# Six of the eight block products of each MLP as seven half-width products of a Strassen scheme

## The chip, the cores and the metric

The kernel runs on one core of a Trainium2 chip. The metric is the device time of one execution in microseconds. Five engines work side by side and meet only at semaphores: TensorE (PE, with its weight loads listed as PEld), VectorE (DVE), ScalarE (ACT), GpSimd (POOL), and SyncE (SP), which issues the weight transfers.

## The reference

A stack of transformer layers over 512 tokens of width 1024: two mixers of a first block, then a second block of two layers, each with a mixer and an MLP, and a last norm. All of it is fp32. The change touches only the two MLPs of the second block:

```
def sq_relu_mlp(h, w_up, w_down):            # w_up 1024 x 4096, w_down 4096 x 1024
    u = jnp.einsum('btd,df->btf', h, w_up)
    return jnp.einsum('btf,fd->btd', jnp.square(jax.nn.relu(u)), w_down)

h = h + sq_relu_mlp(rms_norm_2(h, mlp_norm_g[layer]), mlp_w_up[layer], mlp_w_down[layer])
```

## The kernel before

The activations lie in SBUF transposed: X holds the residual as 8 tiles of 128 features by 512 tokens. A matrix product in nearly full fp32 precision is made of three fp32r matmuls: each operand is split into a high part (rounded to fp32r) and a low part (the rest), and `three` issues high·high, low·high and high·low (L288, L289, L290) into one PSUM bank.

An MLP is cut into four chunks of 1024 hidden features. A chunk is one "up" product (1024 x 1024 weights on HH and HL, the normed input) and one "down" product (1024 x 1024 weights on the hidden tiles). So one MLP is eight block products, in the order up 0, up 1, down 0, up 2, down 1, up 3, down 2, down 3. Each product is 8 output tiles (`tile_t`), each tile 8 tiles of the contraction times 3 matmuls: 24 matmuls of 128x128 weights by 512 columns. L is the layer, c the chunk, m the tile.

Each output tile needs one block of weights of 128 x 1024 values (512 KB). SP loads it into one of two buffers WRAW (`load`); ACT rounds it to WH (`split_high`, L256); DVE subtracts to WL (`split_low`, L265). Both wait until TensorE has used the block three before, so a block is made ready within the time of the tiles ahead of it.

For an up tile DVE evicts relu(bank)·RS to TMP (L2293), ACT squares it and rounds it to a high part (L2316, L2320), and POOL subtracts to get the low part (L2339). For a down tile DVE adds the bank to X (`add_x`, L482). Eight PSUM banks are taken in turn. The up product of the next chunk stands between an up product and the down product that reads its hidden tiles.

Each engine runs its instructions strictly in the order in which its function (`mlp_tensor`, `mlp_vector`, `mlp_scalar`, `mlp_gpsimd`) issues them. SP takes the blocks in the order of a list, `plan`.

Of the kernel before, what the change touches and what calls it, by code (L numbers as in the profile page):

```python
# [8 lines left out]
F32 = mybir.dt.float32  # L9
# [6 lines left out]
T = 512  # L16
# [8 lines left out]
NR, NS = 2, 3  # L25
LAMBDA_INIT = 0.8 - 0.6 * math.exp(-0.3)
# [9 lines left out]
for _n, _w in (("l0", 8), ("l1", 8), ("qa", 2), ("kva", 1), ("qn", 1), ("qr", 1), ("qrs", 1), ("kn", 1), ("kr", 1),  # L36
# [3 lines left out]
    GAIN_W += _w  # L40

# [92 lines left out]
def program(nc, A, out):  # L134
    ctx = ExitStack()
    with ctx:
# [7 lines left out]

        HH = sb("HH", [128, KT, T], FR)
        HL = sb("HL", [128, KT, T], FR)
        WH = [sb(f"WH{i}", [128, BW], FR) for i in range(NS)]
        WL = [sb(f"WL{i}", [128, BW], FR) for i in range(NS)]
# [4 lines left out]
        (yout,) = alias([("yout", [128, KT, T], F32)])  # L153
# [26 lines left out]
        HIDH0, HIDL0, HIDH1, HIDL1 = alias([(f"HID{i}", [128, KT, T], FR) for i in range(4)])  # L180
        HID = [(HIDH0, HIDL0), (HIDH1, HIDL1)]
# [4 lines left out]
        sb("SHARED", [128, 21568])  # L186

        X = sb("X", [128, KT, T])
        WRAW = [sb(f"WRAW{i}", [128, BW]) for i in range(NR)]
        SCR = sb("SCR", [128, 3 * 1280])  # L190
        ST = sb("ST", [128, 512])
# [6 lines left out]
        TMP = sb("TMP", [128, 4, T])  # L198
        EPSC = sb("EPSC", [128, 7])
        ACC = sb("ACC", [128, T])  # L200
        EHH, EHL = sb("EHH", [128, 2, 62], FR), sb("EHL", [128, 2, 62], FR)
# [3 lines left out]
        TRI = sb("TRI", [128, 256], FR)  # L205
# [30 lines left out]
        stream = A["plan"]  # L236
# [4 lines left out]
        on_pool |= {block[("o_v", b), half] for b in range(1, 4) for half in range(2)}  # L241

        def load(e, w, b):
            if b >= NR:
                w.wait_ge(*at("low", b - NR))
            name, i, width, _ = stream[b]
            e.dma_start(WRAW[b % NR][:, 0:width], A[name][i]).then_inc(*dma(f"s_w{b % NR}"))

        def split_high(e, w, b):
# [4 lines left out]
            if b >= NS:  # L254
                w.wait_ge(*at("used", b - NS))
            e.activation(WH[b % NS][:, 0:n], WRAW[b % NR][:, 0:n], ACT.Copy).then_inc(*inc("s_high", ("high", b)))  # L256

# [74 lines left out]
        def h_lo(k):  # L332
# [1932 lines left out]
        def up_tiles(e, w, L, c, g):  # L2265
            for m in range(8):
# [1004 lines left out]
```

## Time and profile before

| | before |
|---|---|
| median of 3 runs | 1849.88 us (1848.64 to 1854.93) |
| the profiled execution | 1848.76 us, its span 1847.0 us |
| PE busy | 1804.7 us, 98% of the span |
| DVE, ACT, POOL busy | 53%, 43%, 26% |
| granted TensorE clock, mean | 0.998 |
| HBM traffic | 77 GB/s over the span |

The span runs from the first to the last instruction; the 1.8 us between it and the execution's time lie around it. Matmuls are pipelined: the duration listed for one is from its start to its modelled end, and matmuls overlap, so their rate is read from the distance between two starts. "Idle before" is the time in which an engine had nothing under way ahead of an instruction, with the instruction that released it.

### The profile page before, as it was taken

The numbers are of one execution on the slowest core, as the hardware profiler recorded it, in microseconds if no ns is written. First come the engines' busy times: TensorE is split into PE (matmuls) and PEld (weight loads), VectorE is DVE, ScalarE is ACT, GpSimd is POOL, SyncE is SP. The second block draws the span as 40 slices with busy tenths as digits, with TensorE's granted clock in tenths as the row PEclk, the third lists the DMA queues.
The fourth block names the chain that finished last, engine by engine and source line by source line (L and its number), as shares of the span: only waits on it lengthen the run. The fifth ranks groups of instructions, "written<-read, shape, count | busy, mean of one in ns | idle before, by whom it ended". The sixth has DMA issues, their size and how long they took to land.

```text
span 1847.0 us, 24633 instructions
## 1 busy us (share of the span) xinstructions
PE 1804.7 (98%) x9664; PEld 1441.0 (78%) x9668; DVE 981.4 (53%) x1581; ACT 797.4 (43%) x1401; POOL 476.5 (26%) x475
## 2 busy tenths in 40 slices
PE   7999999999999999999999999999999999999997
PEld 6987777776678766677888888888888788888886
DVE  5355556575546688854433434365677653333333
ACT  5236665455435365564441423233445543232412
POOL 0035551101312145560120201005677112010200
PEclk9999999999999999999999999999999999999999
DMA  5221111231012311012222222222222122222222
GB/s 182 93 71 54 48 46 60 82 97 48 23 57 96 124 65 34 30 36 70 91 102 103 92 92 102 103 91 81 81 86 75 57 92 100 96 97 97 95 98 79
DMA packets 44514, 149.10 MB, mean 81 GB/s; under 512 B 6000, under 2 KB 6384, under 8 KB 44400
## 3 DMA queue, kind: packets, MB, share of 16 engines
q1 hardware_dynamic: 44400, 147.53, 23.6%
q8 instruction: 78, 1.28, 0.3%
q14 instruction: 36, 0.29, 0.1%
HBM read 139.64 MB, written 2.10 MB: 77 GB/s over the span
## 4 chain that ended last, share of the span: by engine, by line
PE 87%; DVE 5%; POOL 3%; ACT 3%; issue 2%; DMA 1%; POOLq 0%; SPq 0%; DVEq 0%; ACTq 0%
PE BANK L288 23%; PE BANK L290 22%; PE BANK L289 22%; PE BANK L920 3%; PE BANK L654 2%; PE BANK L1704 1%; PE BANK L1685 1%; PE BANK L1661 1%; PE BANK L977 1%; PE BANK L2499 1%; PE BANK L639 1%; PE BANK L2474 1%; DVE LH L763 1%; POOL LH L885 1%; PE BANK L2462 1%
## 5 line engine op out<-in xcount | busy, mean ns | idle before, releaser
L256 ACT ACTIVATE WH<-WRAW 128x1024 fp32r<-128x1024 f32 x262 | 273.3, 1045 | 452.0 <-PE BANK L290 425.6
L265 DVE TENSOR_TENSOR WL<-WRAW,WH 128x1024 fp32r<-128x1024 f32 (+1 forms) x249 | 326.6, 1312 | 253.1 <-ACT WH L256 252.2
L288 PE MATMUL BANK<-HH,WH 128*128 128x512 f32 x1048 | 422.4, 403 | 11.1 <-DVE WL L265 9.6
L290 PE MATMUL BANK<-HL,WH 128*128 128x512 f32 x1048 | 409.4, 391 | 0.0
L289 PE MATMUL BANK<-HH,WL 128*128 128x512 f32 x1048 | 408.9, 390 | 0.0
L288 PEld LDWEIGHTS BANK<-HH,WH 128*128 128x128 f32 x1048 | 197.4, 188 | 60.5 <-issue 20.6
L290 PEld LDWEIGHTS BANK<-HL,WH 128*128 128x128 f32 x1048 | 197.1, 188 | 42.0
L289 PEld LDWEIGHTS BANK<-HH,WL 128*128 128x128 f32 x1048 | 197.6, 189 | 40.4 <-issue 2.9
L2339 POOL TENSOR_TENSOR HID<-TMP,HID 128x512 fp32r<-128x512 f32 x64 | 82.8, 1293 | 527.1 <-ACT HID L2320 527.1
L288 PE MATMUL BANK<-HID,WH 128*128 128x512 f32 (+1 forms) x520 | 200.8, 386 | 0.0
L290 PE MATMUL BANK<-HID,WH 128*128 128x512 f32 (+1 forms) x520 | 200.6, 386 | 0.0
L289 PE MATMUL BANK<-HID,WL 128*128 128x512 f32 (+1 forms) x520 | 200.6, 386 | 0.0
L482 DVE TENSOR_TENSOR X<-X,BANK 128x512 f32<-128x512 f32 x95 | 65.3, 687 | 230.5 <-PE BANK L290 230.5
L2316 ACT ACTIVATE TMP<-TMP 128x512 f32<-128x512 f32 x64 | 40.5, 632 | 202.7 <-DVE TMP L2293 202.7
L288 PEld LDWEIGHTS BANK<-HID,WH 128*128 128x128 f32 x520 | 97.7, 188 | 19.7
L290 PEld LDWEIGHTS BANK<-HID,WH 128*128 128x128 f32 x520 | 97.7, 188 | 19.7
L289 PEld LDWEIGHTS BANK<-HID,WL 128*128 128x128 f32 x520 | 97.7, 188 | 19.6
L2293 DVE SCALAR_TENSOR_TENSOR TMP<-BANK,RS 128x512 f32<-128x512 f32 x64 | 44.2, 690 | 59.4 <-PE BANK L290 59.3
L875 POOL TENSOR_TENSOR L0P<-TMP,L0P 128x512 fp32r<-128x512 f32 x16 | 35.3, 2205 | 146.0 <-DVE L0P L750 146.0
L885 POOL TENSOR_TENSOR LH<-SCR,LH 128x512 fp32r<-128x512 f32 (+1 forms) x48 | 54.0, 1124 | 41.7 <-DVE LH L763 41.7
L2104 ACT ACTIVATE SCR<-BANK,ST 128x512 f32<-128x512 f32 (+3 forms) x96 | 49.6, 525 | 20.1 <-DVE ST L1885 19.9
L2774 ACT ACTIVATE SCR<-BANK,ST 128x128 f32<-128x128 f32 (+3 forms) x64 | 33.1, 522 | 56.8 <-DVE ST L2639 56.8
(413 smaller groups left out, 3113.6 us busy)
## 6 DMA issues: line engine op xcount, KB each, us to landing
WRAW<-in_w SPq DMA_DIRECT2D x77, 512.0 KB, 3.4
WRAW<-in_wu SPq DMA_DIRECT2D x64, 512.0 KB, 3.2
WRAW<-in_wd SPq DMA_DIRECT2D x64, 512.0 KB, 3.2
WRAW<-in_w0o SPq DMA_DIRECT2D x8, 512.0 KB, 3.5
WRAW<-in_w1o SPq DMA_DIRECT2D x8, 512.0 KB, 3.4
WRAW<-in_wc SPq DMA_DIRECT2D x8, 512.0 KB, 3.2
WRAW<-in_w2o SPq DMA_DIRECT2D x8, 512.0 KB, 3.2
WRAW<-in_w3o SPq DMA_DIRECT2D x8, 512.0 KB, 3.2
```

The costliest lines, as they stand in the source:

```text
L256: e.activation(WH[b % NS][:, 0:n], WRAW[b % NR][:, 0:n], ACT.Copy).then_inc(*inc("s_high", ("high", b)))
L265: e.tensor_tensor(WL[b % NS][:, 0:n], WRAW[b % NR][:, 0:n], WH[b % NS][:, 0:n].bitcast(F32), ALU.subtract).then_inc(*inc("s_low_pool" if p ...
L288: e.matmul(dst, ah, bh, start=first and i == 0, stop=False)
L289: e.matmul(dst, al, bh, start=False, stop=False)
L290: made = e.matmul(dst, ah, bl, start=False, stop=last and i == len(sets) - 1)
L482: e.tensor_tensor(X[:, m, :], X[:, m, :], banks[name, m], ALU.add).then_inc(*inc("s_evac", ("evac", name, m)))
L885: e.tensor_tensor(LH1[:, h % 2, c], l0_buf[h % 3][:, c], LH0[:, h % 2, c].bitcast(F32), ALU.subtract).then_inc(*inc("s_fail_lo", ("fail lo ...
L920: made = e.matmul(bank[:, c], a, b, start=(i == 0), stop=(i == len(sets) - 1), skip_group_check=True)
L2104: e.activation(e_exp(u)[:, b, 0:n], BANK[2 * (u % 2) + b][:, 0:n], ACT.Exp, bias=e_stat(u, b), accum_out=e_stat(u, 2 + b)).then_inc(*inc(" ...
L2293: e.scalar_tensor_tensor(out=TMP[:, t % 4, :], in0=banks[("up", L, c), m], scalar=0.0, in1=RS[:, :], op0=ALU.max, op1=ALU.mult).then_inc(* ...
L2316: e.activation(t, t, ACT.Square).then_inc(*inc("s_hid", ("hid square", L, c, m)))
L2339: e.tensor_tensor(lo[:, m, :], TMP[:, (8 * c + m) % 4, :], hi[:, m, :].bitcast(F32), ALU.subtract).then_inc(*inc("s_hid_lo", ("hid lo", L, ...
```

## The change

In each MLP the products up 0 and down 3 stay as they are; the six between them run in the order down 0, up 1, down 1, up 2, down 2, up 3 and by another scheme. Such a product takes its weights, its input and its output as 2x2 blocks (feature tiles k and k+4, output tiles m and m+4, token halves of 256) and computes the 2x2 block product with seven block products in place of eight (a Strassen scheme in Winograd's form).

A step (`FAST`, 48 per MLP) is one pair of output tiles (m, m+4) and one half of the contraction. Per step:

- SP loads the four weight quarters of 128 x 256 (512 KB in all) into one of three buffers RAW (`fast_load`).
- POOL makes four sums of 256 columns from them (`fast_sums`). The second waits for the first, the fourth for the second.
- ACT rounds seven operands of 256 columns in one instruction of 1792 columns (`fast_high`); DVE subtracts in one of 1792 (`fast_low`). RAW and the split operands G have three buffers each.
- TensorE runs 7 products times 2 tiles times 3 matmuls of 256 columns (`fast_pe`), 42 in all, into four banks of a pair; two pairs share the eight banks in turn.

After both steps of a pair, ACT copies one product out of PSUM (256 columns, `first_act`) and DVE joins the seven products in four instructions (512, 512, 256 and 512 columns, `join_vec`) in the one buffer Q. For a down pair POOL adds two tiles of 512 to X (`add_pool`). For an up pair DVE makes relu and square in one pass of 1024 columns (`relu_vec`); the input sums of the next down product come from POOL in three instructions of 512, 256 and 256 (`hid_mix`), then ACT rounds 1792 columns and DVE subtracts 1792 (`hid_high`, `hid_low`). Hidden planes of chunk 3 need no sums and are 1024 wide. The input of the up products, X·gain·RS, is staged and summed once per MLP in four planes (`stage_vec`, two DVE instructions of 512; `plane_mix` like `hid_mix`; `plane_high`, `plane_low`, 1792 columns each): two planes during up 0, two during down 0.

The up 0 tiles run in the order 0, 4, 1, 5, 2, 6, 3, 7, and the product after them is down 0, where before it was up 1. The square of up 0 stays on ACT.

```
+        def fast_sums(e, w, L, s):
...
+            w.wait_ge(*dma(f"s_raw{s % 3}", L * NF // 3 + s // 3 + 1))
+            a21, a11, a12, a22, s1, s3, s2, s4 = (raw_part(s, i) for i in range(8))
+            e.tensor_tensor(s1, a21, a22, ALU.add).then_inc(*inc("s_fast_sum", ("first sum", L, s)))
+            e.tensor_tensor(s3, a21, a11, ALU.subtract).then_inc(*inc("s_fast_sum", ("third sum", L, s)))
+            w.wait_ge(*at("first sum", L, s))
+            e.tensor_tensor(s2, s1, a11, ALU.subtract).then_inc(*inc("s_fast_sum", ("second sum", L, s)))
+            w.wait_ge(*at("second sum", L, s))
+            e.tensor_tensor(s4, a12, s2, ALU.subtract).then_inc(*inc("s_fast_sum", ("sums", L, s)))
...
+        def fast_low(e, w, L, s):
...
+            w.wait_ge(*at("fast high", L, s))
+            e.tensor_tensor(flat(fast_w(s)[:, 7:14, :]), raw_part(s, 1, 7), flat(fast_w(s)[:, 0:7, :]).bitcast(F32),
+                            ALU.subtract).then_inc(*inc("s_fast_low", ("fast low", L, s)))
+        def turn_pool(e, w, S, *key):
+            e.tensor_tensor(S[:, 0:2, :], S[:, 7:8, :].broadcast_to([128, 2, 256]), S[:, 5:7, :], ALU.subtract).then_inc(
+                *inc("s_mixed", ("first mix", *key)))
...
+            e.tensor_tensor(S[:, 2, :], S[:, 5, :], S[:, 1, :], ALU.subtract).then_inc(
+                *inc("s_mixed", ("second mix", *key)))
...
+            e.tensor_tensor(S[:, 3, :], S[:, 4, :], S[:, 2, :], ALU.subtract).then_inc(
+                *inc("s_mixed", ("mixed", *key)))
...
+        def fast_pe(e, w, L, s):
...
+            w.wait_ge(*at("fast low", L, s))
+            wh, wl = fast_w(s)[:, 0:7, :], fast_w(s)[:, 7:14, :]
+            started = set()
+            for name in LATE if kind == "dn" and pair < 2 and half else FIRST:
+                a, b, j, side = PRODUCTS[name]
+                for i in range(2):
...
+                    e.matmul(dst, wh[:, a, cols], hi, start=half == 0 and j not in started, stop=False, skip_group_check=True)
+                    started.add(j)
+                    e.matmul(dst, wl[:, a, cols], hi, start=False, stop=False, skip_group_check=True)
+                    made = e.matmul(dst, wh[:, a, cols], lo, start=False, stop=half == 1 and i == 1, skip_group_check=True)
...
+        def relu_vec(e, w, L, c, p):
...
+            q = flat(Q[:, 0:4, :])
+            e.scalar_tensor_tensor(out=flat(D[:, 4:8, :]), in0=q, scalar=0.0, in1=q, op0=ALU.max, op1=ALU.mult).then_inc(
+                *inc("s_hid_square", ("hid square", L, c, p)))
+
+        def add_pool(e, w, L, c, p):
...
+            e.tensor_tensor(X[:, p + 4, :], X[:, p + 4, :], flat(Q[:, 0:2, :]), ALU.add).then_inc(*inc("s_x_added"))
+            e.tensor_tensor(X[:, p, :], X[:, p, :], flat(Q[:, 2:4, :]), ALU.add).then_inc(
+                *inc("s_x_added", ("x added", L, c, p)))
```

The loop over the steps s on DVE and POOL, in the order of issue ("now", "last", "before" and "third" are the pairs that ended at step s, s-1, s-2 and s-3):

```
+            for s in range(NF + 1):
+                now, last, before, third = (ended.get(s - i, ("", 0, 0)) for i in range(4))
+                if last[0]:
+                    join_vec(e, w, L, *last, 3)
+                if third[0] == "up" and third[1] < 3 and third[2] < 3:
+                    hid_low(e, w, L, *third[1:])
+                if last[0] == "up":
+                    relu_vec(e, w, L, *last[1:])
...
+                fast_low(e, w, L, s + 2)
...
+                if now[0]:
+                    for i in (1, 2, 4):
+                        join_vec(e, w, L, *now, i)
...
+            for s in range(NF + 1):
+                last = ended.get(s - 1, ("", 0, 0))
+                fast_sums(e, w, L, s + 3)
+                if s == 0:
+                    hid_mix(e, w, L, 0, 3)
+                if last[0] == "up" and last[1] < 3:
+                    hid_mix(e, w, L, *last[1:])
+                if last[0] == "dn":
+                    add_pool(e, w, L, *last[1:])
+                if s in (2, 4):
+                    plane_mix(e, w, L, s // 2 + 1, D)
```

## Rows read from the trace of the kernel before

**Rows 1.** The page: busy time by engine, and the granted clock in 40 slices.

```profile
PE 1804.7 (98%) x9664; PEld 1441.0 (78%) x9668; DVE 981.4 (53%) x1581; ACT 797.4 (43%) x1401; POOL 476.5 (26%) x475
PEclk9999999999999999999999999999999999999999
```

**Rows 2.** The page: the chain that ended last, shares by engine.

```profile
PE 87%; DVE 5%; POOL 3%; ACT 3%; issue 2%; DMA 1%; POOLq 0%; SPq 0%; DVEq 0%; ACTq 0%
```

**Rows 3.** Windows over the first MLP: busy PE, PEld, DVE, ACT, POOL, clock, DMA.

```profile
879.20:966.20 87.00, 87.00 (x384) 71.63 (x383) 39.05 (x41) 36.76 (x50) 19.42 (x15) 1.00 0.26 91
966.20:1009.70 43.50, 43.50 (x194) 36.02 (x193) 15.55 (x16) 9.64 (x10) 1.29 (x1) 1.00 0.31 109
...
1140.20:1183.70 43.50, 43.50 (x193) 36.02 (x192) 15.55 (x16) 9.64 (x10) 1.29 (x1) 1.00 0.31 109
```

**Rows 4.** Timeline of TensorE, end of the second MLP: 512 columns, then 256.

```profile
1821.88 0.39 PE L290 MATMUL BANK<-HID,WH 128*128 128x512 f32 x1
...
1829.36 0.39 PE L290 MATMUL BANK<-HID,WH 128*128 128x512 f32 x1
1829.59 0.28 PE L288 MATMUL BANK<-HID,WH 128*128 128x256 f32 x1
...
1833.78 0.28 PE L290 MATMUL BANK<-HID,WH 128*128 128x256 f32 x1
```

**Rows 5.** Timelines of TensorE and DVE: start of up 0, first eviction.

```profile
878.39 0.39 PE L288 MATMUL BANK<-HH,WH 128*128 128x512 f32 x1
...
889.76 0.69 DVE L2293 SCALAR_TENSOR_TENSOR TMP<-BANK,RS 128x512 f32<-128x512 f32 x1
```

**Rows 6.** Instructions of single lines: duration in ns, least, median, most.

```profile
L265 DVE TENSOR_TENSOR WL<-WRAW,WH x249: 407/1226/2353, 8.3 to 1820.1; 128x1024 fp32r<-128x1024 f32 x121, 128x704 fp32r<-128x704 f32 x4
L482 DVE TENSOR_TENSOR X<-X,BANK x95: 680/687/690, 299.4 to 1829.8; 128x512 f32<-128x512 f32 x95
L2339 POOL TENSOR_TENSOR HID<-TMP,HID x64: 1290/1290/1307, 891.9 to 1750.3; 128x512 fp32r<-128x512 f32 x64
L2320 ACT ACTIVATE HID<-TMP x64: 631/632/633, 891.1 to 1749.6; 128x512 fp32r<-128x512 f32 x64
```

**Rows 7.** Groups by line and shape, with mean ns of one.

```profile
L256 ACT ACTIVATE WH<-WRAW 128x1024 fp32r<-128x1024 f32 x65 | 68.4, 1053 | 127.0 <-PE BANK L290 127.0
L455 DVE TENSOR_TENSOR RS<-RS,TMP 128x512 f32<-128x512 f32 x1 | 0.7, 692 | 0.0
```

**Rows 8.** Timeline, DVE and POOL: a DVE instruction with one SBUF input beside POOL.

```profile
1836.39 2.10 POOL L2993 TENSOR_TENSOR yout<-yout,RS 128x256 f32<-128x256 f32 x3 [84.80 <-ACT RS L2967]
1836.74 2.04 DVE L2983 SCALAR_TENSOR_TENSOR yout<-X,GC,BANK 128x256 f32<-128x256 f32 x5
```

**Rows 9.** Timeline, DVE and POOL: DVE instructions with two SBUF inputs beside POOL.

```profile
133.62 1.21 DVE L265 TENSOR_TENSOR WL<-WRAW,WH 128x1024 fp32r<-128x1024 f32 x1
133.77 1.65 POOL L885 TENSOR_TENSOR LH<-SCR,LH 128x256 fp32r<-128x256 f32 x1 [0.23 <-DVE LH L763]
...
187.21 1.23 DVE L265 TENSOR_TENSOR WL<-WRAW,WH 128x1024 fp32r<-128x1024 f32 x1
187.29 2.28 POOL L875 TENSOR_TENSOR L0P<-TMP,L0P 128x512 fp32r<-128x512 f32 x1 [4.21 <-DVE L0P L750]
...
1350.24 1.28 POOL L2855 TENSOR_TENSOR TMP<-TMP,ROPE 128x512 f32<-128x512 f32 x1
1350.42 2.18 DVE L265 TENSOR_TENSOR WL<-WRAW,WH 128x1024 fp32r<-128x1024 f32 x1
1351.47 2.28 POOL L2881 TENSOR_TENSOR OG3L<-OX,OG3H 128x512 fp32r<-128x512 f32 x1
```

**Rows 10.** The page: DMA issues of the MLP weights, us to landing.

```profile
WRAW<-in_wd SPq DMA_DIRECT2D x64, 512.0 KB, 3.2
```

**Rows 11.** Windows where TensorE is partly idle.

```profile
603.00:606.00 3.00, 2.40 (x17) 1.88 (x16) 2.45 (x2) 0.42 (x1) 2.87 (x3) 1.00 0.51 175
1836.00:1840.00 4.00, 1.50 (x8) 0.69 (x6) 3.39 (x9) 2.01 (x5) 2.62 (x4) 1.00 0.00 0
```

More of the change, by code:

```diff
@@ new lines, in mlp_tensor, with part @@
+            for s in range(NF):
+                fast_pe(e, w, L, s)
+            def part(m, ks):
+                b = block[("dn", L, 3), m]
+                wh, wl = (x[b % NS][:, 0:BW].rearrange("p (k n) -> p k n", k=KT) for x in (WH, WL))
+                w.wait_ge(*at("high", b))
+                w.wait_ge(*at("low", b))
+                if ks[0] == 0:
+                    _, was = banks.take((("dn", L, 3), m), ("evac", ("dn", L, 3), m))
+                    for key in was:
+                        w.wait_ge(*at(*key))
+                made = three(e, w, banks[("dn", L, 3), m],
+                             [(wh[:, k, :], wl[:, k, :], dn_plane(k, 0), dn_plane(k, 1), [("hid lo", L, 3, k % 4)]) for k in ks],
+                             ks[0] == 0, ks[-1] == 7)
+                if ks[-1] == 7:
+                    made.then_inc(*inc("s_tile", ("tile", ("dn", L, 3), m), ("used", b)))
@@ L2304, in mlp_vector @@
+            hid_low(e, w, L, 3, 3)
+            split_low(e, w, block[("dn", L, 3), 2], False)
             if L == 0:
@@ new lines, in mlp_scalar @@
+            for s in range(NF + 1):
+                now, last, before = (ended.get(s - i, ("", 0, 0)) for i in range(3))
+                if s == 1 or before[0] == "up" and before[1] < 3 and before[2] == 3:
+                    hid_high(e, w, L, before[1], 3, 1)
+                fast_high(e, w, L, s + 2)
+                if s >= NF - 1:
+                    split_high(e, w, block[("dn", L, 3), s - NF + 1])
+                if s == 0 or last[0] == "up" and last[1:] != (3, 3) and last[2] == 3:
+                    hid_high(e, w, L, last[1], 3, 0)
+                if before[0] == "up" and (before[2] < 3 or before[1] == 3):
+                    hid_high(e, w, L, *before[1:])
+                if s in (3, 5):
+                    plane_high(e, w, L, (s + 1) // 2, D)
+                if now[0]:
+                    first_act(e, w, L, *now)
@@ L3035, in sync @@
             o_swaps = {block[o_slots[s]] + NS + NR: s for s in o_swapped}
-            for b in range(NR, len(stream)):
+            for _, _, _, key in plan[NR:]:
+                if key[0] == "fast":
+                    fast_load(e, w, *key[1:])
+                    continue
+                b = block[key]
                 for pair in m_swaps.get(b, ()):
```

391 lines of the change are left out of this document (306 added, 85 removed).

## The prediction

> **What bounds the kernel now.** I read the page's busy times first: PE is busy 98% of the span and nothing else over 53%, at full clock in every slice [rows 1]. The chain that ended last runs through PE for 87% [rows 2]. Windows over the first MLP show PE without a gap: each block product of 8 tiles takes 43.5 us, so a tile takes 5.44 us, while DVE works 15.6 to 17 us and POOL 1.3 to 9 us of such a window [rows 3]. So an MLP costs what its matmuls cost. Their rate is the distance between starts, not the listed duration: 33 matmuls of 512 columns from 1821.88 to 1829.36 are 0.2267 us each; 35 of 256 columns from 1829.59 to 1833.78 are 0.1197 us [rows 4]. Twice the columns cost 1.89 times as much, so halving the width loses a little.
>
> **TensorE after the change.** A step has 42 matmuls of 256 columns: 42 x 0.1197 = 5.03 us, where an old tile is 24 x 0.2267 = 5.44 us. There are 96 steps in the two MLPs, so if TensorE stays the bound the change gives 96 x 0.41 = 39 us and no more. TensorE no longer hides as much, though, so the question is whether the others keep up with 5.03 us a step, 10.06 us a pair.
>
> By the Trainium skill, "TensorE: Matmul & The Clock Gate", section "Back-to-back issue gap", a matmul costs its columns at the full clock plus a small constant, 109 ns for 256 and 216 ns for 512 columns; by that page's figures the step would save 0.59 us, 57 us in all. The rows of this case say less, and they decide.
>
> **What the helpers do in a step.** Durations first. DVE with both inputs in SBUF: 1.226 us for 1024 columns [rows 6], 0.692 for 512 [rows 7], that is 1.043 ns a column; so 1792 columns take 2.03. POOL: 1.29 us for 512 columns [rows 6], three of 256 in 2.10 us, 0.70 each [rows 8]. ACT: 0.632 for 512, 1.053 for 1024 [rows 6, 7], so 1.68 for 1792.
>
> - ACT, per up pair: two weight roundings, one hidden rounding, one copy under 0.63: at most 5.7 of 10.06 us. Hidden.
> - DVE, per up pair: two `fast_low` and a `hid_low` of 2.03, `relu_vec` 1.23, joins of 1792 columns from PSUM in four instructions, 0.69 for each of 512 [rows 6] and some 0.4 for that of 256: 6.09 + 1.23 + 2.5 = 9.8 us. Just under TensorE, if nothing else holds it. A down pair has 6.6.
> - POOL: eight sums of 0.70 = 5.6; plus `hid_mix` 1.29 + 2 x 0.70 = 2.69, or `add_pool` 2 x 1.29 = 2.58: 8.3 us a pair. Also under.
> - DMA: the same 512 KB per step as per tile, 3.2 us to land [rows 10], three buffers. The engines' share was 0.24 to 0.31 [rows 3]. Nothing changes.
>
> Each engine alone would fit. But DVE and POOL do not run side by side here. When a DVE instruction with two SBUF inputs meets a POOL instruction that reads SBUF, the second one stands still until the first is over [rows 9]: DVE from 187.21 to 188.44, and POOL, started at 187.29, ends 2.28 us later where it needs 1.29, that is 1.13 after DVE's end. At 1350.24 POOL, DVE and POOL come in turn: POOL ends 1351.52, DVE 1.08 later (its 1024 columns), the next POOL instruction 1.15 after that. In the whole trace I found over a hundred such meetings, and none in which the two overlapped. DVE instructions with one SBUF input are free of it: five with a PSUM input beside three of POOL, both at their usual pace [rows 8]. Before, the meetings are rare and lie under PE. The change puts almost all of its new work on these two engines: sums, mixes, additions to X on POOL; subtractions and the relu (both inputs Q, in SBUF) on DVE. Only the joins, which read PSUM, go beside POOL.
>
> So the sum that counts is the time in which one of the two excludes the other. Behind a POOL instruction, a DVE one costs 0.15 less than alone: 1.08 for 1024 columns, 1.88 for 1792, 0.54 for 512. A POOL one behind DVE costs 0.14 less (1.15 for 1.29). I take the first for all DVE instructions, and the second once per DVE instruction.
>
> - Down pair: 5.6 + 2 x 1.88 + 2.58 - 2 x 0.14 = 11.7 us.
> - Up pair (up 1, up 2): 5.6 + 3 x 1.88 + 1.08 + 2.69 - 4 x 0.14 = 14.5 us.
> - Before, the two tiles: 10.88 us. TensorE's part now: 10.06 us.
>
> Both kinds of pair are bound by DVE and POOL together.
>
> **The sum for one MLP**, from the first eviction. That comes 11.4 us after up 0 has begun, since it waits for the norm's factor [rows 5]; this part is not changed.
>
> - During up 0: five mixes 13.5; seven subtractions of 1792 (three hidden planes, two input planes, steps 0 and 1) 13.2; staging of two planes 2.2; five `split_low` 5.4; sums of three steps 8.4: 42.7 us.
> - After it: sums of 45 steps 126.0; 46 `fast_low` 86.5; 12 `add_pool` 31.0; eight up pairs' mix, relu, subtraction 5.65 each, 45.2; four pairs of up 3 with 1024 columns twice 8.6; input planes 2 and 3 11.3; the last plane of up 0 4.6: 313.2 us.
> - Less 0.14 for each of 94 DVE instructions: 13.2. Total 342.7 us.
>
> Before, this stretch (first eviction to the start of down 3) is 7 x 43.5 = 304.5 less 11.4: 293.1 us. The difference is 49.6 us. Two terms are not in it. The work is not wholly without idle: at each of the three hand-overs to a down product the last hidden plane goes through a join, the plane before it, relu, mix behind a step's sums, rounding and subtraction, 0.69 + 2.03 + 1.23 + 2.69 + 2.8 + 1.68 + 2.03 = 13.2 us against two steps of cover, 10.1, so some 3.1 us each, 9.4; dependent POOL instructions leave short gaps, 80 of them, no row of before shows this pair of operations, and I take 0.05 each, 4 us. And the last step's matmuls outlast the helpers by about 2. So 49.6 + 9.4 + 4 + 2 = 65 us per MLP, 130 for both: 1848.8 + 130 = **1979 us**, against the profiled execution's 1848.76, which is 1.1 below the median of 1849.88.
>
> The down 3 product should lose nothing: its first block waits for step 46, the second for the last step, rounding 1.05 and subtraction 1.23 behind join and relu come 3.5 us after it, under the first part's 18 matmuls, 4.1 us. The wait of SP for `fast low` 47 in front of these loads holds only blocks that are needed a step later.
>
> **The ends.** Low: every POOL instruction (264 per MLP, not 94) costs 0.14 less and nothing idles: 24 less, so 49.6 - 24 + 2 = 28 per MLP, 1904 us. High: full durations on both sides (94 x 0.29 = 27 more) and twice the idle (27): 49.6 + 27 + 27 + 2 = 106 per MLP, 2060 us. I take the middle values since the two engines will mostly wait in turn, and that is what the row at 1350.24 shows.
>
> By the Trainium skill, "SBUF — State Buffer", section "Who interferes with whom", the pair of ports is held exclusively for the whole of an instruction. Taken literally, whole durations add, which is my high end without the extra idle; the rows agree with the exclusion but show 0.14 to 0.15 us of each instruction outside it, and I go by them.
>
> **Rivals.**
>
> *TensorE stays the bound* (the other side: faster). If a wide subtraction and a short POOL sum could interleave, each engine alone fits: 9.8 and 8.3 us under 10.06. Then 1848.8 - 39 = 1809, plus some 5 us at each down 0, whose hidden planes had a whole up 1 as cover before and have none now: 1819 us. For it: busy shares of 53% and 26%. Against it: rows 9. It decides from the point where the excluded time per MLP, 343 + 15, falls under 293, that is if 65 us of it can overlap. 0.12.
>
> *A draw*: part of it overlaps and ends about where it was, 1850. 0.03.
>
> *The single buffer D*: relu of the next plane waits until this one is mixed, rounded and subtracted. Unhindered the loop is 1.23 + 2.69 + 1.68 + 2.03 = 7.6 us, but `fast_low` (2.03) and a step's sums (2.8) stand in the two queues and DVE and POOL exclude each other inside it, up to some 17 us a pair in place of 14.5: eight pairs x 2.5 x 2 MLPs = 40 us more, 2019. Inside my range. 0.10.
>
> *The clock*: TensorE would idle a fifth of the time in these stretches (5.03 of about 6.3 us a step). At 1.2 GHz 256 columns are 213 ns and a step 9.0 us: 96 x (9.0 - 5.44) = +342, some 2190 us. Against it: at 80% and at 38% busy the granted clock stayed 1.00 [rows 11]. 0.03.
>
> *The forecast*: 0.72.
>
> **Range and chances.** Forecast and D together hold 0.82 between 1904 and 2060; the range is 1900 to 2060. A measurement of this kernel tells 0.3% from no change, 5.5 us. Faster 0.12, same 0.03, slower 0.85.
>
> **What the profile after would show.** PE busy well under 98%, its gaps in front of the first matmul of a step with `fast_low` on DVE as releaser; 42 matmuls 0.12 apart inside a step; up products longer than down products, some 58 against 47 us; `fast_low` at about 2.03 us at best with a mean above 2.4; POOL sums with a mean over 0.8 and some near 2.6, when they stand behind a subtraction; DVE's joins at their usual 0.69. The clock at 1.00. I am wrong if PE runs through the fast products without gaps, if sums and subtractions overlap at their own durations, or if the waits in front of a step name the DMA or ACT.

## The result and the profile after

The changed kernel took 1995.25 us (median of four runs, 1994.8 to 1996.09), the kernel before 1849.41 (median of four): 1.078 times as long, with an interval of 1.0761 to 1.0803, 146 us more. The forecast was 1979 (1900 to 2060), slower with a chance of 0.85.

The page of the changed kernel, busy times, then the granted clock in 40 slices, and the chain that ended last by engine:

```profile
PE 1827.0 (92%) x11392; PEld 1529.3 (77%) x11396; DVE 1263.5 (63%) x1763; ACT 868.2 (44%) x1383; POOL 1037.2 (52%) x939
...
PEclk9999999999999999998988989999999979899999
...
PE 51%; POOL 26%; DVE 13%; ACT 5%; issue 4%; DMA 1%; DVEq 0%; POOLq 0%; SPq 0%; ACTq 0%
```

Beside [rows 1] and [rows 2]: PE fell from 98% to 92% of a longer span, POOL's busy time more than doubled, and POOL and DVE, 8% of the chain before, now make 39% of it. No single helper is full: 63% and 52%. Only their sum is large, and in the MLPs it is above 100% where busy time includes waiting for each other.

Windows of the first MLP, one for each product from up 0 to up 3 (up 2 and down 2, 54.60 and 51.85 us long, repeat up 1 and down 1). Columns: stretch, length, busy time of PE, PEld, DVE, ACT, POOL, granted clock, DMA share, GB/s.

```profile
881.50:945.84 64.34, 47.58 (x196) 37.36 (x194) 39.45 (x35) 24.48 (x25) 36.77 (x31) 0.89 0.21 69
945.84:996.73 50.89, 43.97 (x337) 43.63 (x337) 36.78 (x28) 20.09 (x17) 48.95 (x38) 0.90 0.23 73
996.73:1051.21 54.48, 45.02 (x336) 44.29 (x337) 37.99 (x30) 17.83 (x13) 51.21 (x43) 0.91 0.26 78
1051.21:1103.09 51.88, 45.80 (x337) 45.06 (x338) 35.38 (x28) 16.70 (x15) 49.78 (x43) 0.90 0.25 82
...
1209.54:1257.24 47.70, 42.73 (x339) 42.01 (x337) 35.72 (x32) 16.98 (x16) 32.44 (x28) 0.96 0.27 86
```

Every product took 43.5 us before [rows 3], up 0 some 44.5 with the matmuls for the norm's factor in it. The six products of an MLP that have 42 matmuls a step now take 47.7 to 54.6 us, where 8 x 5.03 = 40.3 would do for TensorE, and POOL is busy for 94 to 96% of the windows from down 0 to down 2. The product ahead of them, up 0, whose matmuls are not changed, takes 64.3.

From the start of up 0 (881.49) to the start of down 3 (1257.24) the first MLP needs 375.8 us, against 305.6 before (878.39 to 1183.98): +70.2. The second needs 374.6, against 305.6: +69.0. Up 0 of the first MLP starts 3.1 us later than before, 2.7 us are lost between the start of the first down 3 and the second up 0, and 1.1 behind the start of the second down 3 (56.5 us to the end, against 55.5). 3.1 + 70.2 + 2.7 + 69.0 + 1.1 = 146.

The costliest groups that bear on it: busy total, mean ns of one, idle before them and its releaser. `fast_low` is L2361, the fourth of `fast_sums` L2344, the first L2339, the first operation of the mixes L2365, the first addition to X L2525, relu L2516, the joins L2491 to L2499.

```profile
L2361 DVE TENSOR_TENSOR G<-RAW,G 128x1792 fp32r<-128x1792 f32 x96 | 229.6, 2406 | 95.8 <-ACT G L2354 95.7
L2354 ACT ACTIVATE G<-RAW 128x1792 fp32r<-128x1792 f32 x96 | 163.2, 1700 | 270.2 <-POOL RAW L2344 254.8 <-PE BANK L2460 15.4
L2344 POOL TENSOR_TENSOR RAW<-RAW 128x256 f32<-128x256 f32 x96 | 144.2, 1502 | 7.5
L2339 POOL TENSOR_TENSOR RAW<-RAW 128x256 f32<-128x256 f32 x96 | 100.4, 1046 | 0.0
L2365 POOL TENSOR_TENSOR TMP<-TMP 128x512 f32<-128x512 f32 x28 | 65.4, 2334 | 144.9 <-ACT TMP L2627 129.8 <-DVE TMP L2516 13.9 <-DVE TMP L2383 1.3
L2525 POOL TENSOR_TENSOR X<-X,Q 128x512 f32<-128x512 f32 x24 | 45.3, 1887 | 0.0
L2516 DVE SCALAR_TENSOR_TENSOR TMP<-Q 128x1024 f32<-128x1024 f32 x24 | 35.0, 1460 | 1.7
L2491 DVE TENSOR_TENSOR Q<-Q,BANK 128x512 f32<-128x512 f32 x48 | 33.0, 688 | 4.2
```

The means tell who meets whom. A POOL sum of 256 columns needs 0.70 us [rows 8] and the fourth one takes 1.50 on average; where it takes 2.4, as at 1137.11 below, a subtraction on DVE runs beside it. POOL's 512 columns need 1.29 [rows 6] and take 2.33 and 1.89. DVE's 1792 columns, 2.03 at best, take 2.41, and the relu 1.46 for 1.23. The joins, one input in PSUM, stay at 0.69. ACT, which rounds what the POOL has summed, waits 254.8 us for that fourth sum.

The timeline of an up pair in up 2, DVE and POOL in order of time:

```profile
1134.90 0.69 DVE L2491 TENSOR_TENSOR Q<-Q,BANK 128x512 f32<-128x512 f32 x1
...
1139.02 1.56 DVE L2516 SCALAR_TENSOR_TENSOR TMP<-Q 128x1024 f32<-128x1024 f32 x1
1140.50 5.03 DVE L2361 TENSOR_TENSOR G<-RAW,G 128x1792 fp32r<-128x1792 f32 x2
...
1134.89 0.74 POOL L2339 TENSOR_TENSOR RAW<-RAW 128x256 f32<-128x256 f32 x1
...
1137.11 2.38 POOL L2344 TENSOR_TENSOR RAW<-RAW 128x256 f32<-128x256 f32 x1
1140.65 2.99 POOL L2365 TENSOR_TENSOR TMP<-TMP 128x512 f32<-128x512 f32 x1 [1.16 <-DVE TMP L2516]
1143.72 2.40 POOL L2368 TENSOR_TENSOR TMP<-TMP 128x256 f32<-128x256 f32 x1
1146.20 0.73 POOL L2371 TENSOR_TENSOR TMP<-TMP 128x256 f32<-128x256 f32 x1
```

This is [rows 9] again, now in a steady rhythm. Two subtractions take 5.03 us together instead of 4.06, and the 256 columns that start at 1143.72 beside the second of them take 2.40, where the next ones, with DVE idle, take 0.73. A join and a POOL sum that start together, at 1134.9, both keep their own durations (0.69 and 0.74). So the sentence at the start of this document, that the engines meet only at semaphores, does not hold for DVE and POOL.

The chain that ended last, over a down pair (from the addition to X of down 1's third pair to that of its fourth, which runs on POOL while TensorE has begun up 2) and an up pair in up 2 (start, us, what):

```profile
1102.82 1.25 POOL X L2525
1104.07 1.26 POOL X L2526
1105.33 2.48 POOL RAW L2339
...
1112.21 2.39 POOL RAW L2344
1114.61 1.26 POOL X L2525
...
1134.11 0.70 DVE Q L2486
...
1136.64 2.28 DVE HID L2424
...
1139.02 1.57 DVE TMP L2516
...
1140.65 3.00 POOL TMP L2365
...
1145.53 3.49 issue
1149.02 0.70 DVE Q L2486
```

A down pair is POOL from end to end, 11.8 us (1102.82 to 1114.61), two of its ten POOL instructions stretched to 2.4 by a subtraction; an up pair is 14.9 us (1134.11 to 1149.02), passed back and forth between the two engines. In the first MLP no piece of the chain belongs to TensorE from 888.13, under up 0, to 1245.61, in the last quarter of up 3.

From the timeline one can also add up the time in which neither a POOL instruction nor a DVE instruction with two SBUF inputs is under way. An instruction that stands still while the other works adds nothing to such a union, so what is left over is what the pair of engines, taken as one, has free:

| stretch | length, us | free for both, us |
|---|---|---|
| up 0 from the first eviction (892.96 to 945.84) | 52.9 | 8.0 |
| down 0, up 1, down 1 | 50.9, 54.5, 51.9 | 0.9, 0.6, 0.4 |
| up 2, down 2 | 54.6, 51.9 | 0.6, 0.4 |
| up 3 | 47.7 | 5.4 |

In the five products in the middle the two engines together are full to 98 or 99%, at 63% and 52% busy each over the span.

### The profile page after: what moved, and what is told of

It is laid out like the page before. It is cut to its first block, busy times and chain, and to the rows that moved or that the text cites. A ratio compares the mean times of both kernels' runs of the same rounds, so it can differ in the third digit from the quotient of the medians.

```text
span 1993.0 us, 28779 instructions
## 1 busy us (share of the span) xinstructions
PE 1827.0 (92%) x11392; PEld 1529.3 (77%) x11396; DVE 1263.5 (63%) x1763; ACT 868.2 (44%) x1383; POOL 1037.2 (52%) x939
## 4 chain that ended last, share of the span: by engine, by line
PE 51%; POOL 26%; DVE 13%; ACT 5%; issue 4%; DMA 1%; DVEq 0%; POOLq 0%; SPq 0%; ACTq 0%
PE BANK L314 11%; PE BANK L316 10%; PE BANK L315 10%; POOL RAW L2344 5%; POOL RAW L2339 4%; POOL RAW L2342 3%; POOL TMP L2365 3%; POOL RAW L2340 2%; PE BANK L948 2%; PE BANK L682 2%; DVE HID L2424 2%; POOL X L2526 2%; POOL X L2525 2%; POOL TMP L2368 2%; PE BANK L1732 1%
## 5 line engine op out<-in xcount | busy, mean ns | idle before, releaser
L314 PE MATMUL BANK<-HH,WH 128*128 128x512 f32 x664 | 278.3, 419 | 18.1 <-DVE WL L291 9.3
L282 ACT ACTIVATE WH<-WRAW 128x1024 fp32r<-128x1024 f32 (+2 forms) x166 | 172.4, 1041 | 270.7 <-PE BANK L316 225.6
L2361 DVE TENSOR_TENSOR G<-RAW,G 128x1792 fp32r<-128x1792 f32 x96 | 229.6, 2406 | 95.8 <-ACT G L2354 95.7
L2354 ACT ACTIVATE G<-RAW 128x1792 fp32r<-128x1792 f32 x96 | 163.2, 1700 | 270.2 <-POOL RAW L2344 254.8
L2457 PE MATMUL BANK<-HID,G 128*128 128x256 f32 x672 | 202.4, 301 | 72.8 <-DVE TMP L2568 25.5
L316 PE MATMUL BANK<-HL,WH 128*128 128x512 f32 x664 | 264.8, 399 | 0.0
L291 DVE TENSOR_TENSOR WL<-WRAW,WH 128x1024 fp32r<-128x1024 f32 (+2 forms) x153 | 192.7, 1260 | 102.4 <-ACT WH L282 101.1
L2457 PE MATMUL BANK<-HP,G 128*128 128x256 f32 x672 | 197.9, 295 | 46.5 <-DVE G L2361 43.5
L2459 PE MATMUL BANK<-HID,G 128*128 128x256 f32 x672 | 199.7, 297 | 0.0
L2460 PE MATMUL BANK<-HID,G 128*128 128x256 f32 x672 | 199.3, 297 | 0.0
L2457 PEld LDWEIGHTS BANK<-HID,G 128*128 128x128 f32 x672 | 139.0, 207 | 77.8 <-issue 32.5
L2459 PE MATMUL BANK<-HP,G 128*128 128x256 f32 x672 | 195.6, 291 | 0.0
L2460 PE MATMUL BANK<-HP,G 128*128 128x256 f32 x672 | 195.0, 290 | 0.0
L314 PEld LDWEIGHTS BANK<-HH,WH 128*128 128x128 f32 x664 | 126.6, 191 | 56.5 <-issue 28.5
L2344 POOL TENSOR_TENSOR RAW<-RAW 128x256 f32<-128x256 f32 x96 | 144.2, 1502 | 7.5
L2365 POOL TENSOR_TENSOR TMP<-TMP 128x512 f32<-128x512 f32 x28 | 65.4, 2334 | 144.9 <-ACT TMP L2627 129.8
L2459 PEld LDWEIGHTS BANK<-HID,G 128*128 128x128 f32 x672 | 139.0, 207 | 0.0
L2460 PEld LDWEIGHTS BANK<-HID,G 128*128 128x128 f32 x672 | 138.9, 207 | 0.0
```

The source lines that it names most:

```text
L291: e.tensor_tensor(WL[b % NS][:, 0:n], WRAW[b % NR][:, 0:n], WH[b % NS][:, 0:n].bitcast(F32), ALU.subtract).then_inc(*inc("s_low_pool" if p ...
L314: e.matmul(dst, ah, bh, start=first and i == 0, stop=False)
L316: made = e.matmul(dst, ah, bl, start=False, stop=last and i == len(sets) - 1)
L2344: e.tensor_tensor(s4, a12, s2, ALU.subtract).then_inc(*inc("s_fast_sum", ("sums", L, s)))
L2354: e.activation(flat(fast_w(s)[:, 0:7, :]), raw_part(s, 1, 7), ACT.Copy).then_inc(*inc("s_fast_high", ("fast high", L, s)))
L2361: e.tensor_tensor(flat(fast_w(s)[:, 7:14, :]), raw_part(s, 1, 7), flat(fast_w(s)[:, 0:7, :]).bitcast(F32), ALU.subtract).then_inc(*inc("s_ ...
```

## The experiments

The kernel before took 1849 to 1850 us beside each. e1 and e2 were timed once; for the others the ratio to the kernel before is given with its interval. The edits are against the changed kernel. Product lengths are of the first MLP. "Free" is the time defined above.

**e1: the same instructions with one input in SBUF.** The first question was whether it is the two SBUF inputs that cost, or the mere number of instructions, waits and hand-overs.

```diff
-            e.tensor_tensor(flat(fast_w(s)[:, 7:14, :]), raw_part(s, 1, 7), flat(fast_w(s)[:, 0:7, :]).bitcast(F32), ALU.subtract)...
+            if s < 3:
+                ...                                   # the subtraction, as it was, and return
+            ...                                       # a wait for the step before
+            e.tensor_reduce(BEHIND[:, 0:7], RAW[s % 3][:, 1:8, :], AX.X, ALU.add)...
...
+            if c in (1, 2):                           # in hid_low
+                e.tensor_reduce(BEHIND[:, 8:8 + n], D[:, cut, :], AX.X, ALU.add)...
```

> The subtraction of the weights' low parts (from step 3 on) and that of the hidden low parts of chunks 1 and 2 are replaced on VectorE by a reduction over the same 1792 columns: the low parts stay what they were, so the output is not the reference's. Length, order and waits on VectorE stay, but the instruction has one SBUF input where it had two. Exclusion theory (an instruction with two SBUF inputs and one of GpSimd stand still for each other): GpSimd's sums fall to 0.73 us each, both kinds of pair become bound by TensorE at 10.1 to 10.5 us where down pairs took 13 and up pairs 13.6, some 65 us less per MLP, about 1865 us in all. Rival, VectorE alone has too much to do or the chain of hand-overs is too long: nothing changes, since every duration stays, about 1995 us. Rival, GpSimd alone is the bound: its idle time stays near zero and the time stays above 1950 us.

Measured: 1865.04 us. The groups of DVE's reduction and of two of the sums, and the windows of up 1 and down 1:

```profile
L2367 DVE TENSOR_REDUCE JUNK<-RAW 128x7 f32<-128x1792 f32 x90 | 181.5, 2017 | 52.9 <-ACT G L2355 51.4
L2345 POOL TENSOR_TENSOR RAW<-RAW 128x256 f32<-128x256 f32 x96 | 79.9, 832 | 7.5
L2340 POOL TENSOR_TENSOR RAW<-RAW 128x256 f32<-128x256 f32 x96 | 72.4, 755 | 21.7 <-DMA RAW<-in_wf 21.7
```

```profile
988.13:1028.99 40.86, 40.48 (x338) 40.31 (x337) 33.41 (x30) 18.13 (x15) 34.57 (x43) 1.00 0.35 104
1028.99:1070.90 41.91, 41.10 (x336) 40.52 (x337) 33.30 (x31) 18.55 (x16) 36.37 (x46) 1.00 0.36 114
```

The work on DVE is as long as before, 2.017 us an instruction, and stands in the same place of the same queue; POOL has all its sums, mixes and additions. The second SBUF input is gone, and with it 130 of the 146 us. A reduction also writes next to nothing, so this run alone doesn't part the second read from the wide write. The joins do, as far as 512 columns go: they write 512 columns of SBUF from one SBUF input and neither they nor the sums beside them are stretched. TensorE is busy for 40.5 of 40.9 us in up 1, and the sums are back at 0.75 and 0.83. The 16 us left are the balance of up 0, still 64.3 us (2 x 19.8 = 40 more than before; what it does on the helpers is not edited here), and what the six products now win (43.5 against 42.0, 40.9, 41.9 and three of 40.3: 15 per MLP, 31 in all), with 7 us ahead of the first up 0, between the MLPs and at the end, as in the changed kernel.

**e2: no sums on POOL.** If the excluded times simply add, taking the largest of them away must leave TensorE as the bound.

```diff
+            if s > 2:                                 # in fast_sums, ahead of its four instructions
+                return
```

> GpSimd's four sums per step are left out from step 3 on (the rounding takes what lies in the buffer), so the output is not the reference's. Exclusion theory: 2.8 us per step leave the excluded time, up pairs have 9.4 us of it left, so TensorE is the bound in all fast products, about 1860 us. Rival, VectorE alone is the bound: 1995 us. If TensorE is the bound in both this run and the one with one input, neither engine alone is too slow and it is the two together.

Measured: 1917.55 us, better by 78, but 58 above what was expected. Up 1 and up 2 take 45.9 and 44.1 us, the downs 47.2 to 47.6, and only up 3 has TensorE's 40.3. The timeline shows why the sum did not do:

```profile
1071.65 3.01 POOL L2527 TENSOR_TENSOR X<-X,Q 128x512 f32<-128x512 f32 x1 [2.67 <-DVE Q L2501]
...
1077.82 0.69 DVE L2488 TENSOR_TENSOR Q<-Q,BANK 128x512 f32<-128x512 f32 x1 [1.29 <-POOL X L2528]
```

The first addition to X, 1.29 us of work, starts as soon as the joins are done, which is also when DVE starts its next subtraction. It needs 3.01, and the joins of the next pair wait for the additions. Of up 1's 45.9 us 14.3 are free. The exclusion is there even where the two engines have time to spare: it then lengthens a loop of joins, additions and joins.

**e3: relu and square on ACT, in two passes**, as a test of whether a microsecond of DVE's excluded work is worth a microsecond.

```diff
-            e.scalar_tensor_tensor(out=flat(D[:, 4:8, :]), in0=q, scalar=0.0, in1=q, op0=ALU.max, op1=ALU.mult)...
+            e.activation(d, flat(Q[:, 0:4, :]), ACT.Relu)...      # in ACT's queue, ahead of its roundings
+            ...
+            e.activation(d, d, ACT.Square)...
```

> ReLU and square of the fast up products go to ScalarE as two passes of 1024 columns (2.1 us), instead of one pass of VectorE with two SBUF inputs. Exclusion theory: 1.08 us less per up pair, 24 pairs, so about 26 us less, 1969 us. Rival, the loop over the single buffer D (relu, mix, rounding, subtraction) is the bound of the up products: it gets 1 us longer per pair, 2015 us.

Measured: 2001.39 us (1.0817, 1.0801 to 1.0833), 6 us worse. Up 1 and up 2 are nearly unchanged (54.2 and 54.3 us) though DVE has 1.23 us less in each pair, and up 3 rose from 47.7 to 49.1. Two passes of 1.07 us stand in place of one of 1.23 in the chain from join to mix:

```profile
1138.67 1.07 ACT TMP L2516
...
1139.76 1.07 ACT TMP L2518
```

In up 2 the work of the two engines did fall, by 2.1 us over its four pairs, but the free time rose from 0.6 to 2.3: the lighter sum brought 0.3 us, because the longer loop through the single D stood right behind it. From down 0 to down 3 the six products took 1.0 us less in the first MLP (310.4 against 311.4) and 1.5 less in the second, where 13 each had been expected. The 6 us that the run lost don't lie there: they lie in down 3, 2.1 us longer in the first MLP and 5.1 in the second. It had no gap in the changed kernel and now has one of 1.85 us, in the second MLP of 3.33. TensorE goes out of work there because ACT rounds the second block of weights only behind its two passes, and DVE subtracts only then, until 1263.91:

```profile
1261.61 1.04 ACT L282 ACTIVATE WH<-WRAW 128x1024 fp32r<-128x1024 f32 x1
...
1264.01 0.47 PE L314 MATMUL BANK<-HID,WH 128*128 128x512 f32 x1 [1.85 <-issue]
```

**e4: the additions to X on DVE.**

```diff
                 if last[0] == "dn":
-                    add_pool(e, w, L, *last[1:])      # in POOL's queue
+                    add_pool(e, w, L, *last[1:])      # in DVE's queue
```

> The addition of a down pair to X goes from GpSimd (2 x 1.29 us) to VectorE (2 x 0.69 us, of which 0.54 each excludes GpSimd). Exclusion theory: a down pair falls from 11.7 to 5.6 + 3.76 + 1.08 - 0.42 = 10.0 us, that is to TensorE's 10.1, 1.5 us in 24 pairs, about 38 us less, 1957 us. Rival, VectorE is the one that has too much to do: 1.4 us more per down pair, 2025 us.

Measured: 1964.52 us (1.0621, 1.0603 to 1.0639), 31 better than the change. An addition costs DVE less than POOL even with the waiting in it:

```profile
L2526 DVE TENSOR_TENSOR X<-X,Q 128x512 f32<-128x512 f32 x24 | 27.2, 1134 | 0.0
L2525 DVE TENSOR_TENSOR X<-X,Q 128x512 f32<-128x512 f32 x24 | 20.2, 841 | 0.8
```

0.84 and 1.13 us against 1.89 for L2525 on POOL. The down products hardly moved, 50.4 to 50.6 us; the gain showed a product later, in up 1 (49.5), up 2 (51.3) and up 3 (42.2).

**e7: the copy `first_act` ahead of `hid_high` in ACT's queue.** In the chain above, DVE's join at 1149.02 waits 3.49 us; ACT does the copy ahead of that join behind its rounding, which waits for the mix.

```diff
+                if now[0]:
+                    first_act(e, w, L, *now)
                 ...                                   # hid_high
-                if now[0]:
-                    first_act(e, w, L, *now)
```

> On ScalarE the copy of the first product out of PSUM (first_act) is issued ahead of the rounding of the hidden plane before it, not behind it; nothing else changes, so the excluded time is the same. Loop theory (the up products go by the chain relu, mix, rounding, copy, joins, subtraction, relu, in which the exclusions stand as delays): joins no longer wait for the mix, up pairs fall from 13.6 to about 12.5 us, 16 pairs of chunks 1 and 2, about 18 us less, 1977 us. Sum theory (the excluded time itself fills the up products): no change, 1995 us.

Measured: 1993.28 us (1.0768, 1.0746 to 1.0791), no change. Up 1 and up 2 went to 53.3 and 53.4. The wait is gone: from 1099 to 1157 the chain is POOL alone, with no pause over 0.07 us. Yet an up pair still takes 14.7 us, against 14.9, and of up 2's 53.4 us 0.5 are free. So the sum is the limit here, and the shorter loop gives 0.2 us a pair; e3 showed the same two limits from the other side.

**e8: e4 and e7 together; e9: also the mixes of chunks 1 and 2 on DVE; e6: also relu and square on ACT.** The edits are those above, and for e9:

```diff
                 if last[0] == "up" and last[1] < 3:
-                    hid_mix(e, w, L, *last[1:])       # in POOL's queue
+                    hid_mix(e, w, L, *last[1:])       # in DVE's queue
```

> Both edits together: the addition to X on VectorE, and the copy ahead of the rounding. If the loop is what binds the up products, the gains add: 1964.5 - 18 = 1947 us. If the excluded time binds them, 1964 us as with the first edit alone.

> As the run before, and the mixes of the hidden planes of chunks 1 and 2 go from GpSimd (2.69 us) to VectorE (0.69 + 2 x 0.42 us). Excluded time per up pair falls by 2.69 - 1.07 = 1.6 us, and the loop loses two hand-overs and GpSimd's queue: up pairs at 11 to 12 us, 16 pairs, 25 us less than the run before, about 1922 us. Rival, VectorE is then the bound (11.3 us of its own per up pair, plus what it waits): no gain, 1947 us or more.

> As the run before, and ReLU and square of the fast up products on ScalarE in two passes. VectorE has 10.1 us of its own per up pair in place of 11.3. If VectorE is the bound of the up products by then, 24 pairs gain 1 us, about 1900 us; if the loop is, it is 1 us longer and the time rises by some 15 us, as it did not fall when this edit was made alone (2001 us).

Measured: e8 1959.36 us (1.0582, 1.0561 to 1.0603); e9 1941.12 (1.0483, 1.0458 to 1.0507); e6 1951.42 (1.054, 1.0518 to 1.0563). e8 is 5 better than e4 and lies between its two expectations, nearer to the sum's. e9 is another 18 better: on DVE a mix of three operations takes 1.11 + 0.85 + 0.84 us, where POOL needed 2.33 for the first alone. Its products are 46.4 to 47.2 us (down), 52.8 and 48.7 (up 1, up 2) and 40.3 (up 3). e6 is 10 worse than e9, and as in e3 nearly all of the loss is in down 3: 50.0 and 49.8 us in the two MLPs, with a gap of 3.40 in each, against 45.0 and 45.3. None comes near 1849. In e9 the POOL has little but its sums left, and they still take 1.53 us for the fourth; of up 1's 52.8 us 2.0 are free, of up 2's 48.7 2.6, so there too the two engines as one set most of the pace:

```profile
L2344 POOL TENSOR_TENSOR RAW<-RAW 128x256 f32<-128x256 f32 x96 | 146.6, 1527 | 7.5
```

**e10: up 0 without the mixes of chunk 0.** This one is about the other loss, the 20 us ahead of down 0.

```diff
+            if c == 0:                                # in hid_mix, ahead of its three instructions
+                return
```

> GpSimd's three mixes of each of the four hidden planes of chunk 0 are left out (ScalarE rounds the plane as soon as it is squared), so the output is not the reference's. The test is of the stretch of up 0, in which TensorE stands still for 20 us per MLP since the evictions are late. If they are late by the chain through the one buffer D (eviction, square, mix, rounding, subtraction, and only then the next eviction), each of three pairs gets 4 us shorter: 12 us less per MLP, 1971 us. If the excluded time fills that stretch, only the mixes' own 2.7 us per pair go, 8 us per MLP, 1979 us. If the stall has another cause (the blocks of weights, the banks), 1995 us.

Measured: 1975.86 us (1.0683, 1.0665 to 1.0701). Up 0 of the first MLP went from 64.3 to 56.3 us, 8.1 less, which is three mixes at their own 2.7 and the figure that was expected of the sum, not the 12 of the loop. The free time behind the first eviction stayed at 8.0 us. Some 12 us above the old 44.5 remain, 10.5 of them TensorE's idle time ahead of down 0.

**e11: `fast_low` in two instructions of 896 columns, e12: the same on top of e9.** If it is the length of one lock that hurts the POOL, two shorter ones help; if the sum counts, they cost.

```diff
-            e.tensor_tensor(flat(fast_w(s)[:, 7:14, :]), raw_part(s, 1, 7), ...)
+            for half in range(2):
+                c = slice(896 * half, 896 * half + 896)
+                e.tensor_tensor(flat(fast_w(s)[:, 7:14, :])[:, c], raw_part(s, 1, 7)[:, c], ...)
```

> The subtraction of the weights' low parts is cut into two instructions of 896 columns. Excluded time is the same; VectorE has one more instruction per step, and a GpSimd instruction that meets it waits at most half as long. Sum theory: no change or 0.15 us more per step, 1995 to 2009 us. If the length of a single exclusion inside the chains is what costs, the up products get 1 us shorter per pair and the hand-overs too, 1970 to 1980 us.

> The best version that these edits give: addition to X and mixes of chunks 1 and 2 on VectorE, the copy ahead of the rounding, and the subtraction of the weights in two halves. If the gains add, 1941 - 12 = 1929 us; if VectorE, with 11.3 us of its own per up pair, has no room for another instruction per step, 1941 us or a little more. Above the kernel before in either case: the stretch of up 0 alone keeps 40 us.

Measured: e11 1983.63 us (1.0725, 1.0709 to 1.0741), 12 better than the change; e12 1954.73 (1.0564, 1.0547 to 1.0582), 14 worse than e9. The groups of e11 in the stretch from up 1 to up 3 of the first MLP:

```profile
L2363 DVE TENSOR_TENSOR G<-RAW,G 128x896 fp32r<-128x896 f32 x78 | 121.9, 1608 | 25.4 <-ACT G L2354 25.4
L2344 POOL TENSOR_TENSOR RAW<-RAW 128x256 f32<-128x256 f32 x38 | 44.1, 1161 | 3.0
```

In this stretch the fourth sum fell from 1.52 to 1.16 us, while each half of the subtraction now takes 1.61, of which less than 1.1 is its own. It fits that the length of a single lock is a part of the cost as long as POOL sets the pace, and that an instruction more per step costs more than it gives once DVE carries the additions and mixes, but neither is shown: e11 fell between its two expectations, and no run parts the two for e12.

## Why the prediction was right, and where it was off

**The mechanism was right, and e1 shows it.** The forecast rested on [rows 9]: a DVE instruction with two SBUF inputs and a POOL instruction exclude each other. The same lengths in the same queues without the second input brought TensorE back as the bound at 1865 us (one run, but the effect is 130 us). That is also the answer to the rival with TensorE as the bound (0.12). Its condition, that sums and subtractions can overlap, isn't met. Its price of 5 us at each down 0 was too low as well: up 0 and its stall cost 19.8 us there, in e1 too.

**Pairs.** A down pair was forecast at 11.7 us and is 11.8 in the chain, an up pair at 14.5 and is 14.9. The gaps ahead of a step's first matmul, `fast_low` as one releaser, its mean above 2.4 (2.41), POOL's sums above 0.8 in the mean (1.05, 0.78, 0.92 and 1.50 for the four) with single ones at 2.4 to 2.5, and joins at 0.69 came as written. "Up 58, down 47" did not: 54.5 and 51.9, since the last up pair's mix, rounding and subtraction are done in the next down product. The sum of the two is 106 against 105.

**The sum for one MLP.** From the first eviction to down 3 it was 342.7 us of excluded work and 15.4 of idle time, 358 us. The first MLP took 364.3, and the trace parts them: 348.1 us in which one of the two engines works, 16.2 free. By stretches (16 of the 94 deductions of 0.14 us fall under up 0, 78 behind it):

| stretch | forecast: work + idle | measured: work + free |
|---|---|---|
| under up 0 | 40.5 + 0 | 44.9 + 8.0 |
| down 0 to up 3 | 302.3 + 15.4 | 303.2 + 8.2 |

For the six products the work was forecast to 1 us, and the idle time twice too high. The step that was mis-sized is the term "during up 0", 12.4 us too low: its work was priced at 4.4 us too little, and its idle time at nothing. I priced it as a sum of excluded work, but there is also a loop through one buffer: D (TMP in the rows) takes the two evictions of a plane, is mixed, rounded and subtracted from, and only then takes the next plane. The two errors cancel in part, so that the total came within 16 us is to some degree luck. DVE's part of the last turn:

```profile
921.29 0.69 DVE L2568 SCALAR_TENSOR_TENSOR TMP<-BANK,RS 128x512 f32<-128x512 f32 x1
927.42 0.68 DVE L2568 SCALAR_TENSOR_TENSOR TMP<-BANK,RS 128x512 f32<-128x512 f32 x1
...
937.37 2.17 DVE L2424 TENSOR_TENSOR HID<-TMP,HID 128x1792 fp32r<-128x1792 f32 x1 [4.49 <-ACT HID L2417]
939.65 0.69 DVE L2568 SCALAR_TENSOR_TENSOR TMP<-BANK,RS 128x512 f32<-128x512 f32 x1
```

From the first eviction of a plane to that of the next the turns take 15.4 us (905.92 to 921.29) and 18.4 (921.29 to 939.65), where TensorE makes the two tiles in 11.2 (48 matmuls 0.2333 apart). In the last turn the mix starts 2.9 us after the eviction's end, behind sums for the fast steps, and its first operation, beside a `fast_low` of 2.50 us, takes 3.04 for 1.29; DVE is idle for 4.49 us ahead of the subtraction. Down 0 waits for the banks: its first matmul comes at 945.84, after 13.33 us of idle, released by the last eviction, that of 944.80. e10 shows the other part: without the mixes the work falls from 44.9 to 36.8 us and the free time stays at 8.0, so a mix counts there as work of the sum. No run here shortens the loop alone, and a second D was not tried.

The 16 us by which 1979 fell short are thus 70.2 + 69.0 - 2 x 65 = 9 in the MLPs and 7 ahead of, between and behind them. (The two stretches behind the first eviction came out 11 us longer than forecast, but I had taken the old ones 0.95 us too short each, without the factor's matmuls, which hid 2.) In the 7 there is a loss of TensorE's pace where nothing of its work was changed: matmuls of 512 columns on HH, HL and the hidden tiles start 0.2333 us apart after the change, from the first mixer on, and 0.2268 before, at a granted clock of 1.00 in both. Down 3 of the first MLP, 192 of them without a gap, takes 44.8 us instead of 43.5: 1.3 of the 2.7 us between the MLPs, and the 1.1 at the end go the same way. Those of the mixers on OG0, OG1 and OG3 stay at 0.227. The change also gives many buffers another place in SBUF, but no run here tests whether that is the cause, and it stays open. The start of the first up 0 moves between runs too, from 880.9 us (e7) to 887.6 (e9) with the same code ahead of it, so a few microseconds between two experiments say little by themselves.

**The single buffer as a loop in up 1 and up 2** I had as a rival with 2.5 us a pair above 14.5. Measured 0.4 a pair above, so it is not dearer than the sum there. But it is as close as that. In the changed kernel the sum leaves 0.6 us of up 2 free; e7 takes the loop out of its way and the pair still needs 14.7; e3 makes the sum lighter and the loop longer, and gets 2.3 us of free time and no shorter product. e4, e8 and e9 gain by taking work from POOL.

**As a model of what an edit is worth, the sum is poor.** It gave 1860 for e2 (1918), 1969 for e3 (2001) and 1922 for e9 (1941). It holds where the two leave nothing free, and stops holding when one is relieved, because a lock that falls into a chain costs its length there even with idle time around it.

**The clock** was forecast at 1.00 and is 0.89 to 0.91 in the windows of most products, so [rows 11] misled me: short idle stretches there had not touched it, and the second of those windows ends at 1840.00, while 0.50 is granted from 1840.1 on. The rival's 2190 us, all at 1.2 GHz, did not come either. In the first MLP no piece of the chain between the first eviction and 1245.61 is TensorE's, so there the lower clock costs nothing that the chain shows. In the last quarter of up 3, where TensorE is on it, some 16 matmuls are 0.21 us apart instead of 0.12: about 1.5 us. In the second MLP TensorE is on the chain for one step of down 2 and the last two of up 3, both at 0.12 us a matmul.

**Down 3 waits for nothing**, as forecast: TensorE has no gap in it in either MLP. It is longer than before by the 0.2333 us alone. e3 and e6 show how narrow the cover was: with two passes more on ACT ahead of it TensorE stood still for 1.9 to 3.4 us.

**Is there a version that wins?** None that ran. Up 3, which has no mixes behind it, reached TensorE's 40.3 us in e9, 3.2 us under the old 43.5. So this product alone, changed in both MLPs, could at most give 6 us, an estimate from these two lengths; it needs the hand-overs to and from the fast form, and it was not built.

## What to carry to other kernels

When matmuls are traded for additions on the vector engines, add up DVE's two-input SBUF instructions and POOL's as if they were one engine; 63% and 52% busy was full, with 1 to 2% free in the products that counted. Then follow each single buffer once round its loop with a stretched duration (own plus the other engine's) for each operation in it, also in the stages ahead of the changed one. If it doesn't fit, move the POOL's operations to DVE (e4, e9) rather than DVE's to a longer way round (e3, e6), and look first for a form with one input in SBUF or one in PSUM.

## What the runs showed of the hardware

**The form of a DVE instruction decides, not its length.** DVE's TENSOR_REDUCE over 1792 columns of SBUF, one input, ran 90 times at 2.017 us with the POOL at work beside it, and the POOL's sums fell to 0.75 and 0.83 us. The subtraction with two inputs had 2.41, the sums up to 1.50. DVE's joins, one input in SBUF and one in PSUM, kept their 0.69 us for 512 columns beside POOL.

**The granted clock falls in gaps of TensorE.** Before, it was 1.00 through the first MLP [rows 3] and 0.9 or more in every slice [rows 1]. After, in the stall ahead of down 0, with TensorE idle since 932.5:

```profile
938.00:942.00 4.00, 0.00 (x0) 0.00 (x0) 2.24 (x2) 1.62 (x2) 4.00 (x4) 0.50 0.00 0
```

That is 1.2 GHz. It also shows in the starts of matmuls a little earlier, behind an idle time of 3.44 us:

```profile
925.13 0.63 PE L314 MATMUL BANK<-HH,WH 128*128 128x512 f32 x1 [3.44 <-issue]
925.55 0.63 PE L315 MATMUL BANK<-HH,WL 128*128 128x512 f32 x1
...
929.09 0.39 PE L315 MATMUL BANK<-HH,WL 128*128 128x512 f32 x1
929.32 0.40 PE L316 MATMUL BANK<-HL,WH 128*128 128x512 f32 x1
```

512 columns are 0.42 us apart at first, and 0.23 from 928.9 on. In the fast products, where TensorE idles for one to a few microseconds ahead of a step, the mean is 0.90, and in e1, where it hardly idles, 1.00.

**The pace of a matmul is not fixed by its columns and the granted clock.** The same 512 columns at a granted clock of 1.00 started 0.2268 us apart in one kernel and 0.2333 in the other, for the same source lines and moved tiles (HH, HL) in mixers that the change does not touch. The cause stays open.
